# Layer 1's first gate-up part placed behind the second tile's transposes, the third tile's transposes inside it

## Chip, cores and metric

One of the cores of a Trainium2 chip runs the whole program. The metric is the device time of one execution in microseconds (us). A core has five engines with their own instruction streams: PE (matmuls and transposes), DVE and ACT (element by element), POOL (here: splitting the weights), and SP (here: starting transfers). They meet only through semaphores.

## What is computed

Two layers over 512 latent tokens and 256 context tokens of 1024 channels. What the change touches is the start of the feed-forward half of a layer:

```python
x = post_norm(x, g1 * y_l, ln1_w[layer], ln1_b[layer])
x = post_norm(x, g2 * swiglu(modulate(x, sh2, sc2), w_gate_up[layer], w_down[layer]),
              ln2_w[layer], ln2_b[layer])

def modulate(x, shift, scale):
    return layer_norm(x) * (1.0 + scale) + shift
def swiglu(h, w_gu, w_dn):
    g, u = jnp.split(h @ w_gu, 2, axis=-1)
    return (jax.nn.silu(g) * u) @ w_dn
```

`w_gate_up` is 1024 x 5632. The second and last layer (layer 1) computes this for the latent tokens only.

## The kernel before

**Tiles.** Tokens go in tiles of 128. Layer 0 has six of them, layer 1 in its feed-forward half four (here called first to fourth, numbered 0 to 3 in the code). Each fp32 product is made of three matmuls (`product`, L658 to L660): high by high, low by high, high by low half of the operands. Weights arrive in `stage`, POOL splits them into the eight slots of `ring_hi` (L623) and `ring_lo` (L626), and the last product that reads a slot raises `ring_used`, which lets POOL fill it again.

**From the norm to the operand.** After the output projection each tile goes through a chain over three engines. DVE adds the residual and norms twice (L1739 to L1812). ACT writes the normed tile `xn` (L1305). PE transposes it in eight blocks of 128 x 128 into two banks (`transposes`, L755). ACT modulates it into `hbuf` (L1313); for the last two tiles DVE does half of this (L1773). ACT writes the high half `act_hi` (L1321) and DVE the low half `act_lo` (L1730), and DVE then raises `low_ready`. PE's `wait_low(pe, key, n)` waits for that of tile n. `xn`, the two banks and `hbuf` are shared by the tiles, so the transposes of tile n wait for `xn` of tile n and for the modulation of tile n - 1. On ACT the order is fixed: modulation of tile n, square root of tile n + 1, high half of tile n, `xn` of tile n + 1.

**The start of gate-up.** `gate_up(l, 0)` (L1098) works on the first two blocks f = 0, 1 of 128 hidden columns in parts of 256 tokens (two tiles), `part(f, r, last)` (L1130): 8 gate products and then 8 up products, 48 matmuls. In layer 1 there are two token ranges r = 0, 1 and so four parts, in the order (f, r) = (0,0), (1,0), (0,1), (1,1), called first to fourth part. Before the parts with f = 0 PE waits for the low half of the second tile of their range: the second tile for the first part, the fourth tile for the third part. Transposes of the first tile stand in the last pass of the output projection (`last_pass`, L1076). Behind the parts come the blocks f = 2, 3, ... for all 512 tokens (`chunk`, L1104). Only parts with r = 1 raise `ring_used`. PE's order is the order in which this code is written; nothing passes a waiting instruction.

**ACT behind the norm.** After the fourth tile's high half, ACT issues two DMAs for the next norm's weights (L1558, L1559) and two for modulation weights (L1594), loads the table for silu and waits for the third part.

Of the kernel before, what the change touches and what calls it, by code (L numbers as in the profile page):

```python
# [136 lines left out]
def build(nc, x, c, ctx_in, c_ctx, w_mod, b_mod, w_in, a_q_norm, a_k_norm, b_sink, f_mix, r_decay,  # L137
# [3 lines left out]
    with stack:  # L141
# [111 lines left out]
        def sem(*name):  # L253
            key = "_".join(str(n) for n in name)
            if key not in sems:
                sems[key] = stack.enter_context(nc.semaphore(key))
            return sems[key]
# [16 lines left out]
        def tiles_of(l):  # L274
            return ALL if l < DEPTH - 1 else LAT
# [55 lines left out]
        def gates_done(l, seg):  # L331

            return GATE_OUT[(l, seg, 1)] + streams_of((l, seg, 1))
# [14 lines left out]
        def gate_banks(l, fh, f):  # L348

            parts = len(token_parts(l))  # L350
            if f % 2:
                return slice(2, 2 + parts), slice(4, 4 + parts)
            return slice(6, 6 + parts), slice(0, parts)
# [8 lines left out]
        def sum_bank(l, fh, f):  # L362

            return gate_banks(l, fh, f)[1].stop - 1

        def part_place(l, f, gu, r):

            c0 = r * 256 + (0 if l < DEPTH - 1 else CTX)
            return ps[:, r + f * len(tiles_of(l)) // 2, gu * 256:gu * 256 + 256], slice(c0, c0 + 256)
# [69 lines left out]
        def ffn_acc(half, n):  # L439

            items = FFN_MODS[half]
            return n % 3 if half == (0, 1) else 0 if items[n][1] != "modC" else 1 + items[n][2]

        def ffn_sum_chunk(half, n):

            last = max(f for f in range(HALF) for _, m, _, part in FFN_WHEN[half][f] if m == n and part == 3)
            return last + 2
# [5 lines left out]
        def ffn_units_to(half, n):  # L453

            return max(u for f in range(HALF) for u, m, _, _ in FFN_WHEN[half][f] if m == n) + 1
# [8 lines left out]
        def wait_low(e, key, n):  # L464

            need(e, "low_ready", key, n + 1)

        def shared_modulation(key, n):

            return n >= len(tiles_of(key[0])) - 2  # L470
# [29 lines left out]
        def need(e, name, l, n):  # L500

            before = NORMS[:NORMS.index(l)] if isinstance(l, tuple) else range(l)
            e.wait_ge(sem(name), n + sum(signals(name, k) for k in before))
# [151 lines left out]
        def _(pe):  # L655
            def product(o, a_hi, a_lo, b_hi, b_lo, first, last):

                nc.tensor.matmul(o, a_hi, b_hi, start=first, stop=False)  # L658
                nc.tensor.matmul(o, a_hi, b_lo, start=False, stop=False)  # L659
                return nc.tensor.matmul(o, a_lo, b_hi, start=False, stop=last)  # L660
# [32 lines left out]
            def column_sums(item, acc, bank, col):  # L693

                n = streams_of(item)
                for q in range(4):
                    for o in range(n):
                        mm = nc.tensor.matmul(ps[:, bank, col + n * q + o:col + n * q + o + 1], acc[:, o, q * P:(q + 1) * P],
                                              ones[:, :], start=(q + o == 0), stop=True, skip_group_check=True)
                mm.then_inc(col_out, 1)  # L700
# [45 lines left out]
            def transposes(key, n):  # L746

                need(pe, "xn_ready", key, n + 1)
                if n > 0:
                    need(pe, "h_ready", key, n)  # L750
                    if shared_modulation(key, n - 1):
                        nt = len(tiles_of(key[0]))
                        need(pe, "h_half", key, signals("h_half", key) - (nt - n))
                for k in range(KC):
                    mm = nc.tensor.transpose(ps[:, 6 + k // 4, (k % 4) * P:(k % 4 + 1) * P], xn[:, n % 2, k * P:(k + 1) * P],  # L755
                                             ident[:, :])
                mm.then_inc(sem("xn_T"), 1)
# [340 lines left out]
            def gate_up(l, fh):  # L1098
                lo_col, width, parts = (0, 384, 2) if l < DEPTH - 1 else (CTX, 512, 1)
                seg = f"gu{fh}"  # L1100
                g0 = SLOT0[(l, seg)]
                f0 = fh * HALF

                def chunk(g, f):  # L1104

                    if f >= 2:
                        need(pe, "hid_ready", l, f0 + f - 1)
                    elif f == 1:
                        need(pe, "dn_read", l, 2 * len(tiles_of(l)))
                    for n, item in enumerate(FFN_MODS[(l, fh)]):  # L1110
                        if item in COL_NO and ffn_sum_chunk((l, fh), n) == f:
                            pe.wait_ge(ffn_mod_used, ffn_units_to((l, fh), n))
                            column_sums(item, mod_acc_ffn[:, ffn_acc((l, fh), n), :, :], sum_bank(l, fh, f), 384 + 16 * (COL_NO[item] % 2))
                    for j in range(4):
                        pe.wait_ge(w_ready, g + j + 1)
                        for q in range(2):
                            k = 2 * j + q
                            for gu in range(2):
                                w = slice(q * 256 + gu * P, q * 256 + (gu + 1) * P)
                                wh, wl = ring_hi[:, (g + j) % RING, w], ring_lo[:, (g + j) % RING, w]  # L1120
                                for r in range(parts):
                                    bank = gate_banks(l, fh, f)[gu].start + r
                                    if f == 0 and k == 0 and gu and l < DEPTH - 1:
                                        need(pe, "dn_read", l, len(tiles_of(l)) + bank + 1)
                                    o = ps[:, bank, 0:width]
                                    s = slice(lo_col + r * width, lo_col + (r + 1) * width)
                                    mm = product(o, wh, wl, act_hi[:, k, s], act_lo[:, k, s], k == 0, k == 7)
                        mm.then_inc(ring_used, 1)

                def part(f, r, last):  # L1130

                    for gu in range(2):
                        o, s = part_place(l, f, gu, r)
                        for j in range(4):
                            g = g0 + 4 * f + j
                            pe.wait_ge(w_ready, g + 1)
                            for k in (2 * j, 2 * j + 1):
                                w = slice(k % 2 * 256 + gu * P, k % 2 * 256 + (gu + 1) * P)
                                mm = product(o, ring_hi[:, g % RING, w], ring_lo[:, g % RING, w], act_hi[:, k, s], act_lo[:, k, s],
                                             k == 0, k == 7)  # L1140
                            if last and gu:
                                mm.then_inc(ring_used, 1)

                if fh == 0:
                    key, nt = (l, 1), len(tiles_of(l))
                    n_parts = nt // 2
                    for n in ([1, 2] if n_parts == 2 else []):
                        transposes(key, n)
                    rest = list(range(3, nt))
                    steps = [(f, r) for r in range(n_parts) for f in range(2)]  # L1150
                    for f, r in steps:
                        if f == 0:
                            wait_low(pe, key, 2 * r + 1)
                            need(pe, "wout_read", l, nt + min(nt, r + n_parts + 1))
                        part(f, r, r == n_parts - 1)
                        if rest:
                            transposes(key, rest.pop(0))
                else:
                    pe.wait_ge(gate_read, gates_done(l, "modC"))
                for f in range(0 if fh else 2, HALF):  # L1160
                    chunk(g0 + 4 * f, f)
# [1074 lines left out]
```

## Time and profile before

| | us |
|---|---|
| median of three runs | 1818.13 (1816.22 to 1820.87) |
| the profiled execution | 1817.81 |
| its span | 1816.0 |
| PE busy | 1695.2 |
| DVE busy | 874.5 |
| POOL busy | 792.0 |
| ACT busy | 459.4 |

Times in the rows below count from the start of the span. A timeline row has start and duration in us, engine, line, operation, result <- operands, their shapes, and how many instructions are merged; in square brackets the idle time of the engine before it and the instruction that ended it. A wait row has who waited for whom, total us, number of waits, the longest. In rows by stretch "PEclk" is the granted clock of PE, 1.00 being the full one (2.4 GHz) and 0.50 the lower one (1.2 GHz). The time from the start of one matmul to the start of the next is what it costs in a dense stream; its duration in the row is longer, since matmuls overlap.

### The profile page before, as it was taken

The page shows a single profiled execution, that of the slowest core. Times are in us where ns is not written, and L with a number is a line of the kernel's source. Part 1 is how long each engine was busy: PE and PEld are TensorE (multiplying, and loading weights), DVE is VectorE, ACT ScalarE, POOL GpSimd, SP SyncE. Part 2 cuts the span into 40 slices and gives each one's busy share as a digit, 9 for nine tenths or more (in the row PEclk, how much of TensorE's full clock was granted, in tenths as well). Part 3 has the DMA queues.
Part 4 walks back from the last instruction along what each step waited for, and adds up shares of the span by engine and source line. Part 5 has one row for each costly group of instructions (what it writes and reads, how often), then busy time and mean ns, then how long its engine had stood idle before and what let it go on. Part 6 is the DMA issues. An engine that isn't in the chain of part 4 may idle for free. (4 is left out here: it accounts for less than half of the span.)

```text
span 1816.0 us, 23167 instructions
## 1 busy us (share of the span) xinstructions
PE 1695.2 (93%) x9198; PEld 1381.8 (76%) x9198; DVE 874.5 (48%) x1264; ACT 459.4 (25%) x956; POOL 792.0 (44%) x780
## 2 busy tenths in 40 slices
PE   5999899999899999999999969898999699999997
PEld 3887666557799997799998758685727688778885
DVE  4353244656862513554454684734476621340048
ACT  5411465521600002100002153126531400210021
POOL 3443001511464543544444444520143497677772
PEclk8999899999989999999999989999999899999999
DMA  9111034302162411244642211210112363233321
GB/s 358 55 57 60 20 127 152 96 1 70 48 185 82 128 60 46 70 123 133 192 156 72 64 46 42 75 47 17 49 50 70 93 174 104 82 93 93 100 98 47
DMA packets 157297, 164.96 MB, mean 91 GB/s; under 512 B 6414, under 2 KB 111742, under 8 KB 156934
## 3 DMA queue, kind: packets, MB, share of 16 engines
q1 hardware_dynamic: 136566, 121.40, 21.6%
q10 hardware_dynamic: 20624, 42.09, 7.0%
q8 instruction: 73, 1.20, 0.3%
q14 instruction: 34, 0.28, 0.1%
HBM read 161.37 MB, written 2.10 MB: 90 GB/s over the span
## 5 line engine op out<-in xcount | busy, mean ns | idle before, releaser
L623 POOL TENSOR_SCALAR ring_hi<-stage 128x512 fp32r<-128x512 f32 x368 | 266.6, 725 | 708.6 <-PE ps L660 680.9
L626 POOL TENSOR_TENSOR ring_lo<-stage,ring_hi 128x512 fp32r<-128x512 f32 x368 | 510.1, 1386 | 30.7
L658 PE MATMUL ps<-act_hi,ring_hi 128*128 128x384 f32 (+2 forms) x1168 | 405.4, 347 | 0.6 <-POOL ring_lo L626 0.6
L659 PE MATMUL ps<-act_lo,ring_hi 128*128 128x384 f32 (+2 forms) x1168 | 403.1, 345 | 0.0
L660 PE MATMUL ps<-act_hi,ring_lo 128*128 128x384 f32 (+2 forms) x1168 | 402.9, 345 | 0.0
L658 PE MATMUL ps<-ring_hi,act_hi 128*128 128x512 f32 (+1 forms) x748 | 298.8, 400 | 17.7 <-DVE act_lo L1730 9.1
L660 PE MATMUL ps<-ring_hi,act_lo 128*128 128x512 f32 (+1 forms) x748 | 291.4, 390 | 0.0
L659 PE MATMUL ps<-ring_lo,act_hi 128*128 128x512 f32 (+1 forms) x748 | 291.2, 389 | 0.0
L658 PEld LDWEIGHTS ps<-act_hi,ring_hi 128*128 128x128 f32 x1168 | 222.5, 190 | 13.9 <-POOL ring_lo L626 0.8
L659 PEld LDWEIGHTS ps<-act_lo,ring_hi 128*128 128x128 f32 x1168 | 222.4, 190 | 12.9
L660 PEld LDWEIGHTS ps<-act_hi,ring_lo 128*128 128x128 f32 x1168 | 222.2, 190 | 13.1
L658 PEld LDWEIGHTS ps<-ring_hi,act_hi 128*128 128x128 f32 x748 | 143.1, 191 | 56.7 <-issue 16.8
L2094 DVE TENSOR_TENSOR hid<-silu_g,ps 128x768 f32<-128x768 f32 (+1 forms) x44 | 36.1, 821 | 308.6 <-ACT silu_g L1580 308.4
L1580 ACT ACTIVATE silu_g<-ps 128x768 f32<-128x768 f32 (+1 forms) x44 | 31.0, 706 | 566.9 <-PE ps L660 525.1
L660 PEld LDWEIGHTS ps<-ring_hi,act_lo 128*128 128x128 f32 x748 | 142.8, 191 | 29.1
L659 PEld LDWEIGHTS ps<-ring_lo,act_hi 128*128 128x128 f32 x748 | 143.2, 191 | 26.9 <-issue 0.5
L1929 DVE SCALAR_TENSOR_TENSOR mod_acc_ffn<-mod_stage,c_silu,mod_acc_ffn 128x512 f32<-128x512 f32 x140 | 131.0, 960 | 26.8 <-DMA mod_stage<-in_w_mod_dram 23.7
L635 POOL TENSOR_TENSOR act_lo<-o_nrm,act_hi 128x128 fp32r<-128x128 f32 x40 | 18.1, 454 | 256.4 <-ACT act_hi L1434 256.4
L1958 DVE TENSOR_REDUCE negmax<-ps 128x1 f32<-128x768 f32 (+4 forms) x80 | 58.0, 766 | 94.3 <-PE ps L874 57.8
L1730 DVE TENSOR_TENSOR hs_lo<-hid,hs_hi 128x768 fp32r<-128x768 f32 (+1 forms) x44 | 59.0, 1341 | 80.1 <-ACT hs_hi L1567 72.1
L658 PE MATMUL ps<-ring_hi,hs_hi 128*128 128x512 f32 x220 | 88.0, 400 | 4.1 <-DVE resid L1741 3.1
L659 PE MATMUL ps<-ring_lo,hs_hi 128*128 128x512 f32 x220 | 86.7, 394 | 0.0
(216 smaller groups left out, 1957.9 us busy)
## 6 DMA issues: line engine op xcount, KB each, us to landing
stage<-in_w_gate_up_dram SPq DMA_DIRECT2D x88, 512.0 KB, 5.0
mod_stage<-in_w_mod_dram ACTq DMA_DIRECT2D x56, 512.0 KB, 4.2
stage<-in_w_in_dram SPq DMA_DIRECT2D x18, 1024.0 KB, 5.1
stage<-in_w_down_dram SPq DMA_DIRECT2D x16, 1024.0 KB, 4.9
stage<-in_w_mod_dram SPq DMA_DIRECT2D x12, 1024.0 KB, 5.3
start_mod<-in_w_mod_dram SPq DMA_DIRECT2D x8, 1024.0 KB, 12.2
stage<-in_w_down_dram SPq DMA_DIRECT2D x8, 768.0 KB, 4.3
stage<-in_w_out_dram SPq DMA_DIRECT2D x16, 256.0 KB, 4.6
```

The lines of the kernel that those rows point to most:

```text
L623: nc.gpsimd.tensor_scalar(ring_hi[:, g % RING, :], stage[:, par, j * 512:(j + 1) * 512], 1.0, 0.0, ALU.mult, ALU.add).then_inc(w_hi, 1)
L626: nc.gpsimd.tensor_tensor(ring_lo[:, g % RING, :], stage[:, par, j * 512:(j + 1) * 512], ring_hi[:, g % RING, :].bitcast(F32), ALU.subtrac ...
L635: nc.gpsimd.tensor_tensor(act_lo[:, ch, c], o_nrm[:, i % 2, :], act_hi[:, ch, c].bitcast(F32), ALU.subtract).then_inc(sem("o_lo"), 1)
L658: nc.tensor.matmul(o, a_hi, b_hi, start=first, stop=False)
L659: nc.tensor.matmul(o, a_hi, b_lo, start=False, stop=False)
L660: return nc.tensor.matmul(o, a_lo, b_hi, start=False, stop=last)
L1580: ins = a.activation(silu_g[:, e, lo_col:TOK].rearrange("p (r n) -> p r n", r=parts if fh or f > 1 else len(tiles_of(l)) // 2), gate_acc(l ...
L1730: return v.tensor_tensor(dst, src, high.bitcast(F32), ALU.subtract)
L1929: return v.scalar_tensor_tensor(acc, w, c_k, acc, ALU.mult, ALU.add)
L1958: v.tensor_reduce(negmax[:, m:m + 1], flat[:, 0:n], AX, ALU.max, negate=True).then_inc(sem("neg_ready"), 1)
L2094: done(v.tensor_tensor(hid[:, j, lo_col:TOK].rearrange("p (r n) -> p r n", **pat), silu_g[:, e, lo_col:TOK].rearrange("p (r n) -> p r n", ...
```

## The change

In layer 1 PE no longer does the third tile's transposes before the first part, but between its gate and its up products. The fourth tile's transposes, which stood behind the first part, now stand behind the second part, right ahead of the wait of the third part. `n_parts` is 2 in layer 1 and 3 in layer 0, where the order stays.

```diff
-                def part(f, r, last):
+                def part(f, r, last, split_at=None):
 
                     for gu in range(2):
+                        if gu and split_at is not None:
+                            transposes((l, 1), split_at)
                         o, s = part_place(l, f, gu, r)
...
                     n_parts = nt // 2
-                    for n in ([1, 2] if n_parts == 2 else []):
-                        transposes(key, n)
+                    if n_parts == 2:
+                        transposes(key, 1)
                     rest = list(range(3, nt))
                     steps = [(f, r) for r in range(n_parts) for f in range(2)]
                     for f, r in steps:
                         if f == 0:
                             wait_low(pe, key, 2 * r + 1)
                             need(pe, "wout_read", l, nt + min(nt, r + n_parts + 1))
-                        part(f, r, r == n_parts - 1)
-                        if rest:
+                        part(f, r, r == n_parts - 1, 2 if n_parts == 2 and f + r == 0 else None)
+                        if rest and (n_parts == 3 or f):
                             transposes(key, rest.pop(0))
```

## Rows read from the trace of the kernel before

**Rows 1.** The page, busy time of each engine, share, instructions.

```profile
PE 1695.2 (93%) x9198; PEld 1381.8 (76%) x9198; DVE 874.5 (48%) x1264; ACT 459.4 (25%) x956; POOL 792.0 (44%) x780
```

**Rows 2.** Waits of PE, 1400 to 1460.

```profile
PE ps L755 <- ACT xn L1305: 15.9, 2, 8.3
```

**Rows 3.** Timeline of PE, 1415 to 1457.

```profile
1420.39 1.97 PE L755 MATMUL ps<-ident_r,xn 128*128 128x128 f32 x8 [8.28 <-ACT xn L1305]
1429.95 1.97 PE L755 MATMUL ps<-ident_r,xn 128*128 128x128 f32 x8 [7.59 <-ACT xn L1305]
1431.57 0.56 PE L658 MATMUL ps<-act_hi,ring_hi 128*128 128x256 f32 x1
1431.93 0.42 PE L659 MATMUL ps<-act_lo,ring_hi 128*128 128x256 f32 x1
...
1434.07 0.31 PE L660 MATMUL ps<-act_hi,ring_lo 128*128 128x256 f32 x1
1434.22 0.28 PE L658 MATMUL ps<-act_hi,ring_hi 128*128 128x256 f32 x1
...
1438.53 1.03 PE L755 MATMUL ps<-ident_r,xn 128*128 128x128 f32 x8
1439.32 0.36 PE L658 MATMUL ps<-act_hi,ring_hi 128*128 128x256 f32 x1
...
1456.66 0.40 PE L658 MATMUL ps<-act_hi,ring_hi 128*128 128x512 f32 x1
```

**Rows 4.** The chain of waits in order of time (start, us, what), 1427 to 1431.

```profile
1427.01 1.24 DVE act_lo L1730
...
1428.66 1.25 ACT xn L1305
```

**Rows 5.** By stretch: length, busy time of the engines, PEclk, DMA share, GB/s.

```profile
1456.60:1750.00 293.40, 290.43 (x1269) 236.83 (x1269) 75.33 (x83) 33.92 (x57) 217.23 (x217) 1.00 0.36 108
```

**Rows 6.** Waits of PE from 1456.6 to the end, the largest.

```profile
PE ps L658 <- DVE resid L1741: 2.0, 2, 1.4
```

**Rows 7.** Timeline of POOL, its first split after the pause.

```profile
1449.07 0.62 POOL L623 TENSOR_SCALAR ring_hi<-stage 128x512 fp32r<-128x512 f32 x1 [22.39 <-PE ps L660]
```

**Rows 8.** By stretch, behind the restart at 1429.95.

```profile
1429.95:1434.15 4.20, 4.20 (x20) 4.20 (x21) 4.06 (x9) 1.68 (x5) 0.00 (x0) 0.50 0.45 119
1434.15:1438.50 4.35, 4.35 (x38) 4.35 (x38) 1.91 (x5) 2.19 (x2) 0.00 (x0) 1.00 0.00 0
```

**Rows 9.** By stretch, behind other restarts of PE.

```profile
38.00:41.60 3.60, 3.59 (x9) 2.86 (x10) 2.03 (x2) 3.57 (x6) 3.52 (x3) 0.52 1.06 381
479.20:485.30 6.10, 6.09 (x29) 6.09 (x30) 5.82 (x8) 4.03 (x10) 3.71 (x3) 0.51 0.16 49
1145.60:1149.00 3.40, 3.40 (x20) 3.00 (x21) 3.19 (x10) 0.49 (x1) 0.00 (x0) 1.00 0.00 0
1236.70:1239.60 2.90, 2.90 (x9) 1.23 (x10) 0.00 (x0) 0.00 (x0) 0.00 (x0) 0.51 0.00 0
```

**Rows 10.** Timeline of PE, those restarts with the idle time before them.

```profile
38.01 0.77 PE L658 MATMUL ps<-ring_hi,act_hi 128*128 128x512 f32 x1 [4.10 <-DVE act_lo L1730]
479.21 1.97 PE L755 MATMUL ps<-ident_r,xn 128*128 128x128 f32 x8 [2.91 <-ACT xn L1305]
1145.57 0.55 PE L772 MATMUL ps<-ident_r,post 128*128 128x128 f32 x3 [2.83 <-DVE post L1855]
1236.67 2.93 PE L874 MATMUL ps<-qk_A 64*128 64x512 f32 x8 [4.35 <-ACT probs L1409]
```

**Rows 11.** Timeline of ACT, 1434 to 1452.

```profile
1435.57 1.23 ACT L1305 ACTIVATE xn<-resid,st 128x1024 f32<-128x1024 f32 x1
...
1443.00 1.28 ACT L1580 ACT_TABLE_LOAD   x1 [0.80 <-issue]
1451.10 0.60 ACT L1580 ACTIVATE silu_g<-ps 128x512 f32<-128x512 f32 x1 [6.83 <-PE ps L660]
```

**Rows 12.** Timeline of DVE, the fourth tile's low half.

```profile
1442.30 1.23 DVE L1730 TENSOR_TENSOR act_lo<-hbuf,act_hi 128x1024 fp32r<-128x1024 f32 x1 [1.27 <-ACT act_hi L1321]
```

## Prediction

> **What bounds the kernel now.** I read the page's busy times first. The reader is to see there one engine near its limit: PE is busy for 93% of the span, DVE, ACT and POOL for at most half [rows 1]. So what counts is where PE stands still or runs at its lower clock, and whether the change alters either. Second, the waits of PE round the start of layer 1's gate-up: two waits for ACT's xn, 15.9 us together [rows 2]. Third, PE's own timeline. The second tile's transposes start at 1420.39 after 8.28 us of idling, the third's at 1429.95 after 7.59 us more; then 192 matmuls of 256 columns (four parts of 48) run without a break, the fourth tile's transposes among them, to 1456.66 [rows 3]. Fourth, the chain of waits: the third tile's transposes hang on xn, which ACT writes from 1428.66 to 1429.91, and that hangs on DVE, which worked on the second tile's low half until 1428.25 [rows 4]. That low half is what the first part needs, and nothing of part one needs the third tile. So PE holds back a part that could start at 1428.3 in order to do transposes that are ready at 1429.95. Behind 1456.66 PE is busy for 290.43 of 293.40 us at full clock [rows 5].
>
> **The change part by part.** Layer 0 has three parts a block and gets neither the split nor another place for its transposes, so its instruction stream stays. In layer 1 nothing is added or removed: the same 192 matmuls and 32 transposes, no DMA, no new tile. Two groups of eight transposes change places, and with them the waits that they carry. Call the tiles first to fourth.
>
> *The first part moves ahead of the third tile's transposes.* It waits for the second tile's low half, which ends at 1428.25 [rows 4]; PE starts within 0.05 us of a release here (xn ends 1429.91, transposes start 1429.95). So it starts at about 1428.3, not at 1429.95 as PE's work does now: 1.65 us gained. Its weights are long there, since POOL sits idle for 22.39 us before 1449.07, with all eight ring slots filled [rows 7]. Bounds: nothing in the rows before this point is touched, so I keep 1.5 to 1.7.
>
> *The clock at that start.* The granted clock is 0.50, the lower of the two levels, from PE's restart at 1429.95 to about 1434.2, and 1.00 behind [rows 8]. Lower-level cost from rows 3: eight transposes take 1.62 (1429.95 to 1431.57) against 0.79 (1438.53 to 1439.32) later; the first 12 matmuls take 2.65 (1431.57 to 1434.22) against 12 x 0.120 = 1.44. Loss now: 0.83 + 1.21 = 2.0. (0.120 is (1456.66 - 1439.32)/144; at the lower level one takes 0.214, (1434.07 - 1431.93)/10.) A stretch at the lower level thus loses 1 - 0.120/0.214 = 0.44 of its length. After other idle stretches the lower level lasted 2.9, 3.6 and 6.1 us from the restart, and 4.3 here [rows 8 to 10]. I take 3.6, from the restart that like the new one begins with full matmuls and not with transposes, for both restarts of the changed kernel: 1.6 lost each time. At the front that is 0.4 less than now. Bounds: 2.9 gives 1.3 (0.7 less than now), 6.1 gives 2.7 (0.7 more).
>
> *The third tile's transposes stand between gate and up products.* They start at 1428.3 + 24 x 0.120 + 1.6 = 1432.8, 2.8 later than now, when xn has been there since 1429.91. They cost their 0.79, counted already. Who waits for them: ACT's and DVE's modulation of the third tile, and queued behind ACT's, the fourth tile's square root and xn. All of it moves by about 2, so that xn of the fourth tile, now 1435.57 to 1436.80 [rows 11], would be there by 1439; it is wanted at 1442.2. Cost nothing, cover 3 us. If that cover were gone, the fourth tile's transposes would come later by what is missing, with PE idle for it.
>
> *The fourth tile's transposes lose their cover.* Now they stand between part one and part two. In the changed kernel they are issued behind part two, and the very next instruction is the third part, which waits for the fourth tile's low half. Now the transposes start at 1438.53 and the low half ends at 1442.30 + 1.23 = 1443.53 [rows 3, 12], so the chain of transposes, modulation on ACT and DVE, high half, low half is 5.00 long. Now part two (5.8) lies over it and part three starts with no wait. After the change the transposes start at 1428.3 + 96 x 0.120 + 0.79 + 1.6 = 1442.2, low is ready at 1447.2, PE is through with its eight at 1443.0: PE stands for 5.00 + 0.05 - 0.79 = 4.3. ACT and DVE have finished the third tile by then and have nothing else to do, so the chain is queued behind nothing and doesn't get shorter. Behind the waiting matmul stand, in PE's order, the whole of parts three and four and all later chunks; nothing can pass. POOL waits for part three's ring releases, and SP's weight loads for POOL; both shift along. On ACT's queue stand, behind the fourth tile's high half, four DMA issues and the table load for silu, now 1443.00 to 1444.28, with the first silu at 1451.10 [rows 11]: they move by 3.7, and so does that silu, so their 6.8 us of cover stay. Bounds: 3.9 to 4.7, an allowance of 0.4 either way on a chain of four steps that has been read once.
>
> *The clock after that stall.* Idle stretches of PE and what followed [rows 9, 10]: 2.83 idle, then 1.00; 2.91 idle, then 0.51; 4.10 idle, then 0.52; 4.35 idle, then 0.51. The new stall of 4.3 is nearest to the last two, so I take a fall, with 3.6 at the lower level: +1.6. Bounds 0 (no fall) to 2.7.
>
> The Trainium skill bears on this term, against the change: its page "TensorE: Matmul & The Clock Gate", section "Why this matters for your kernels", asks for no gaps of idle time between bursts of matmuls, since the gap takes the clock back to half. By that rule the term stands; without it the sum would be 2.2. The trace agrees in three of four gaps.
>
> Sum: -1.65 (earlier start) - 0.4 (front at lower clock) + 4.3 (stall) + 1.6 (clock behind it) = +3.85. As times: parts end at 1428.3 + 192 x 0.1204 + 2 x 0.79 + 1.6 + 4.3 + 1.6 = 1460.5 against 1456.66. What comes after is PE-bound [rows 5]; the longest group of PE's waits in it is 2.0, on residuals for which PE itself releases DVE [rows 6], so nearly all of the shift reaches the end.
>
> The profiled execution took 1817.81 (span 1816.0 and 1.8 round it), 0.3 under the median 1818.13. So 1821.6 in its terms and 1821.9 as median.
>
> **Rivals.**
> *A: the clock stays up over the stall.* For: 2.83 idle left it at 1.00 [rows 9, 10]. Against: the two gaps of 4.1 and 4.35. Gives +2.2, 1820.3.
> *B: both restarts are long ones (slower by over 0.3%).* One mechanism, the clock: at both restarts the lower level lasts 6.1, as after the restart at 479.21 [rows 9, 10], so that part one and the transposes in it run at the lower level altogether, and most of part three too. 3.85 + 1.1 + 1.1 = +6.0, 1824.1. It decides from about 5 us of lower level at both. For: seen once. Against: that restart began with transposes, and 2.9, 3.6 and 4.3 are more frequent.
> *C: the stall does not come up (not slower).* The third part finds the fourth tile's low half ready, or its wait bears on less than I read. Then -1.65 - 0.4 = -2.05, 1816.1. It decides where the chain is below 0.8 instead of 5.0. For: the front's gain is real. Against: each link of the chain has its row, and the wait stands in the code for the third part.
> *D: transposes inside the part run at the lower level.* The eight between gate and up product would take 1.62, not 0.79: 3.85 + 0.83 = +4.7, 1822.8. (The fourth tile's would lengthen chain and stall by what PE works more, so they add their 0.83 at most once more, 1823.6.) Against: the eight at 1438.53, in the middle of dense matmuls, took 0.79 [rows 3].
> The Trainium skill, same page, section "Part 4: PE-mode transpose", says that the full clock is not engaged by transposes. By that rule D would hold; the rows at 1429.95 (1.97 for eight, granted 0.50) and 1438.53 (1.03, granted 1.00) [rows 3, 8] show that transposes do run faster at the granted 1.00, so D stays small.
>
> **How the numbers follow.** Forecast 0.63, A 0.17, B 0.11, C 0.04, D 0.05. The median is from runs that spread from 1816.22 to 1820.87, so some 1.5 either way lies on each. A measurement of this kernel tells a change from about 0.3%, 5.45 us. Slower by more: most of B (0.08), and of the forecast and D the part that lies 1.6 above its value (0.09): 0.17. Faster by more needs -5.45, which no case reaches: 0.02. Within: 0.81. The range goes from A less a spread of the median (1818.7) to B plus a little (1825).
>
> **What would show it.** In the changed trace: first-part matmuls from about 1428.3; no wait of PE for xn of the third tile; transposes of the fourth tile right behind the second part; then a wait of PE for DVE's act_lo of about 4.3 us, a new row; granted clock 0.50 for some 3 to 4 us behind it; matmuls of 512 columns from 1460.5. The prediction is wrong in its mechanism if no such wait appears, and in a size if the chain from the transposes to the low half is not 5.0 or the lower level lasts otherwise.

## Result and profile after

The changed kernel takes 1822.16 us in the median of 18 runs (1819.31 to 1828.35), the kernel before 1818.08 in 18 runs of the same occasions (1815.16 to 1824.99). The ratio is 1.0021, 95% interval 1.0011 to 1.0031: slower by 4.1 us. The interval lies above 1, so the kernel is slower; the size is below the 0.3% from which the prediction counted a change, though the top of the interval lies just over it. Forecast were 1821.9 and +3.85. The profiled execution of the changed kernel has a span of 1819.1.

Spans of single executions scatter by more than the effect: the first tile's transposes, ahead of everything that was changed, start anywhere from 1408.21 to 1416.37 in the twelve profiles of this document. So I compare stretches inside the executions. First the waits of PE in the changed kernel round the start of gate-up, 1400 to 1470 (who waited for whom, total us, times, longest), to be read against [rows 2]. The kernel's line numbers are two higher than before from the new lines on: L1307 is xn, L1732 act_lo.

```profile
PE ps L658 <- DVE act_lo L1732: 10.0, 2, 5.9
PE ps L755 <- ACT xn L1307: 8.3, 1, 8.3
```

Before there were two waits for xn and none for act_lo. One of the two went (7.59), and two waits for low halves came, 5.94 and 4.01. The timeline of PE shows where, against [rows 3]:

```profile
1417.53 1.97 PE L755 MATMUL ps<-ident_r,xn 128*128 128x128 f32 x8 [8.28 <-ACT xn L1307]
1425.43 0.58 PE L658 MATMUL ps<-act_hi,ring_hi 128*128 128x256 f32 x1 [5.94 <-DVE act_lo L1732]
...
1430.72 1.24 PE L755 MATMUL ps<-ident_r,xn 128*128 128x128 f32 x8
1431.71 0.36 PE L658 MATMUL ps<-act_hi,ring_hi 128*128 128x256 f32 x1
...
1440.42 1.03 PE L755 MATMUL ps<-ident_r,xn 128*128 128x128 f32 x8
1445.47 0.58 PE L658 MATMUL ps<-act_hi,ring_hi 128*128 128x256 f32 x1 [4.01 <-DVE act_lo L1732]
...
1459.76 0.40 PE L658 MATMUL ps<-act_hi,ring_hi 128*128 128x512 f32 x1
```

From the second tile's transposes PE works again after 7.90 us (1425.43 - 1417.53); before it was 9.56 (1429.95 - 1420.39). That is the earlier start, 1.66. The fourth tile's transposes start at 1440.42 and the third part at 1445.47, 5.05 later. From the second tile's transposes to the first matmul of 512 columns it takes 42.23 us against 36.27 before, so this one execution lost 5.96 here. Behind it nothing has changed: 1819.1 - 1459.76 = 359.3, before 1816.0 - 1456.66 = 359.3. That the whole span grew by 3.1 only is because this execution reached the place 2.86 earlier. The stretches with their granted clock (third number from the end), against [rows 5, 8]:

```profile
1425.40:1430.70 5.30, 5.27 (x24) 5.27 (x25) 4.55 (x8) 1.24 (x1) 0.00 (x0) 0.50 0.70 193
1430.80:1440.40 9.60, 9.60 (x81) 9.60 (x80) 2.91 (x7) 3.77 (x7) 0.00 (x0) 0.98 0.00 0
...
1445.50:1451.20 5.70, 5.70 (x27) 5.70 (x28) 0.00 (x0) 0.68 (x1) 0.00 (x0) 0.50 0.95 284
1451.30:1459.70 8.40, 8.40 (x71) 8.40 (x71) 2.46 (x3) 0.60 (x1) 7.19 (x8) 0.98 0.12 34
1459.70:1753.10 293.40, 290.43 (x1269) 236.82 (x1269) 75.37 (x83) 33.93 (x57) 217.48 (x217) 1.00 0.37 108
```

The clock is at 0.50 over the whole gate product of the first part and rises only at 1431.1, inside the third tile's transposes, 5.7 us after the first restart; after the second it rises at 1451.6, 6.1 us later. Behind the parts PE's busy time is the same to a hundredth (290.43). DVE, ACT and POOL, against [rows 12, 11, 7], in three views:

```profile
1434.73 1.23 DVE L1732 TENSOR_TENSOR act_lo<-hbuf,act_hi 128x1024 fp32r<-128x1024 f32 x1 [0.59 <-ACT act_hi L1323]
...
1444.19 1.23 DVE L1732 TENSOR_TENSOR act_lo<-hbuf,act_hi 128x1024 fp32r<-128x1024 f32 x1 [1.27 <-ACT act_hi L1323]
```

```profile
1434.52 1.24 ACT L1307 ACTIVATE xn<-resid,st 128x1024 f32<-128x1024 f32 x1
...
1444.89 1.28 ACT L1582 ACT_TABLE_LOAD   x1 [0.81 <-issue]
1454.20 0.60 ACT L1582 ACTIVATE silu_g<-ps 128x512 f32<-128x512 f32 x1 [8.02 <-PE ps L660]
```

```profile
1452.17 0.62 POOL L623 TENSOR_SCALAR ring_hi<-stage 128x512 fp32r<-128x512 f32 x1 [28.35 <-PE ps L660]
```

The fourth tile's xn is there at 1435.76, 4.7 us before its transposes, so the move of the third tile's transposes held nothing up. Its low half ends at 1445.42, and PE starts 0.05 later. POOL is idle six us longer: it waits for PE. The first silu comes later too, after 8.02 us of waiting for PE instead of 6.83, so the cover of what stands ahead of it on ACT has grown.

### The profile page after: what moved, and what is told of

The parts are those of the page before. It is cut to its first block and busy times, and to the rows that moved or that the text cites. A ratio compares the mean times of both kernels' runs of the same rounds, so it can differ in the third digit from the quotient of the medians.

```text
span 1819.1 us, 23167 instructions
## 1 busy us (share of the span) xinstructions
PE 1696.9 (93%) x9198; PEld 1383.9 (76%) x9198; DVE 873.8 (48%) x1264; ACT 459.6 (25%) x956; POOL 792.1 (44%) x780
## 5 line engine op out<-in xcount | busy, mean ns | idle before, releaser
L1732 DVE TENSOR_TENSOR hs_lo<-hid,hs_hi 128x768 fp32r<-128x768 f32 (+1 forms) x44 | 59.0, 1342 | 80.1 <-ACT hs_hi L1569 72.2
```

The costliest lines, as they stand in the source:

```text
L1732: return v.tensor_tensor(dst, src, high.bitcast(F32), ALU.subtract)
```

## Experiments

The theory: the fourth tile's chain (transposes, modulation, high half, low half) has lost its cover and stands on PE's path, and the idle time costs a second time through the clock. The rival: the third tile's transposes inside the first part do the harm. For each kernel the table has the time from the first tile's transposes to the first matmul of 512 columns in its one profile, and the ratio to the kernel before over all runs, the kernel before having been measured again beside each. A stretch is one execution: the two of the changed kernel differ by 1.4 us, so smaller differences between two rows count only where the timeline says what they are made of. The expectations count from the second tile's transposes; the difference to the table is 9.3 us, except in the kernels with extra matmuls at the front, of which more below.

| kernel | stretch, us | less before | ratio, 95% interval |
|---|---|---|---|
| before | 45.58 | | |
| the change | 51.55 | +5.97 | 1.0021, 1.0011 to 1.0031 |
| after_again | 50.11 | +4.53 | 1.0033, 1.0021 to 1.0044 |
| late_alone | 53.00 | +7.42 | 1.0041, 1.0027 to 1.0055 |
| t3_back | 44.88 | -0.70 | 1.0001, 0.9986 to 1.0016 |
| t3_mid | 46.01 | +0.43 | 1.0002, 0.9991 to 1.0013 |
| t3_inside | 43.67 | -1.91 | 0.9974, 0.9960 to 0.9987 |
| t3_inside2 | 43.67 | -1.91 | 0.9980, 0.9970 to 0.9990 |
| busy_stall | 47.97 | +2.39 | 1.0015, 1.0001 to 1.0028 |
| warm_before | 43.91 | -1.67 | 0.9996, 0.9979 to 1.0013 |
| warm_best | 43.53 | -2.05 | 0.9985, 0.9972 to 0.9998 |
| warm_fuller | 42.49 | -3.09 | 0.9977, 0.9963 to 0.9991 |

**late_alone: one half of the change.**

```diff
 # the kernel before
-                        if rest:
+                        if rest and (n_parts == 3 or f):
                             transposes(key, rest.pop(0))
```

> The kernel before with one edit: the fourth tile's transposes behind the second part; the third tile's stay ahead of the first part. Theory (exposed chain): PE stands for 4.3 us before the third part and restarts at the lower clock for 3 to 6 us, so +4.3 +1.3 to +2.7 = +5.6 to +7.0 against before, ratio 1.0031 to 1.0039, slower than the full change, which also has an earlier start. Rival (the split inside the first part is what costs): no wait of PE for act_lo here, ratio 1.000. From the second tile's transposes to the first 512-column matmul: 36.3 before, 42 to 43.3 by the theory.

The loss is there without the split: 1825.66 against 1818.31 for the kernel before. In the stretch it is +7.42, more than the change's +5.97 and +4.53. PE at the third part:

```profile
1446.99 1.03 PE L755 MATMUL ps<-ident_r,xn 128*128 128x128 f32 x8
1452.03 0.58 PE L658 MATMUL ps<-act_hi,ring_hi 128*128 128x256 f32 x1 [4.01 <-DVE act_lo L1730]
```

The same 5.04 from transposes to third part and 4.01 idle. The place of the fourth tile's transposes alone makes the kernel slower; the rival falls. The third and fourth parts took 14.21 us (1452.03 to 1466.24) where 96 matmuls at 0.120 are 11.56, so 2.65 went to the lower clock, as expected. Its 53.00 lies 0.4 over the expected top, and that comes from the front: the first and second parts took 13.25 (1433.74 to 1446.99) where they took 6.96 + 48 x 0.120 = 12.74 before, since the lower clock lasted 5.3 us from the third tile's transposes instead of 4.2. Together 4.25 + 2.65 + 0.5 = 7.4.

**t3_back: the other half.**

```diff
 # the changed kernel
-                        if rest and (n_parts == 3 or f):
+                        if rest:
                             transposes(key, rest.pop(0))
```

> The changed kernel with the fourth tile's transposes back behind the first part, so only the split and the earlier start are left. Theory: no wait of PE for act_lo before the third part. The transposes now wait for the fourth tile's xn, which came 5.04 us after the start of the third tile's transposes, while PE has 3.9 us of work there: a wait of 1.2 us. The first part starts 1.65 sooner. So -1.65 + 1.2, and -0.7 to +0.7 for the clock at the front: -1.2 to +0.3, ratio 0.9993 to 1.0002; the stretch 35.1 to 36.6 us. Rival (the split costs): +4 and the stretch about 40.

PE in the changed place:

```profile
1432.01 1.04 PE L755 MATMUL ps<-ident_r,xn 128*128 128x128 f32 x8
1432.80 0.36 PE L658 MATMUL ps<-act_hi,ring_hi 128*128 128x256 f32 x1
...
1436.90 1.09 PE L755 MATMUL ps<-ident_r,xn 128*128 128x128 f32 x8 [0.99 <-ACT xn L1307]
1437.74 0.36 PE L658 MATMUL ps<-act_hi,ring_hi 128*128 128x256 f32 x1
```

No cost of the split shows: 1819.01 against 1818.31, interval 0.9986 to 1.0016. Its earlier start is partly eaten by the wait for the fourth tile's xn, whose transposes start 1.2 us later than PE's work would have let them (1432.80 + 24 x 0.120 = 1435.69), as expected from the chain ahead. With it neither half of the rival's claim is left.

**t3_inside: cover on both sides.** The fourth tile's transposes after 12 of the second part's 24 gate matmuls.

```diff
 # the changed kernel, inside part, after the matmuls of j
+                            if inside is not None and gu == 0 and j == 1:
+                                transposes((l, 1), inside)
...
-                        part(f, r, r == n_parts - 1, 2 if n_parts == 2 and f + r == 0 else None)
-                        if rest and (n_parts == 3 or f):
+                        part(f, r, r == n_parts - 1, 2 if n_parts == 2 and f + r == 0 else None,
+                             3 if n_parts == 2 and (f, r) == (1, 0) else None)
+                        if rest and n_parts == 3:
```

Here j counts the four ring slots of a product, six matmuls each.

> The changed kernel with the fourth tile's transposes inside the second part, after 12 of its 24 gate matmuls. Theory: xn is there (5.04 after the third tile's transposes start; PE arrives after 5.3), and behind them PE has 36 matmuls = 4.3 us and its own 0.8, against a chain of 5.0: both waits gone. Only the earlier start is left: -1.65, and -0.7 to +0.7 for the clock: -2.4 to -0.9, ratio 0.9987 to 0.9995; the stretch 34 to 35.4 us. Rival (the split costs, or the fourth tile's place is of no matter): as the change, ratio 1.002.

> The same as t3_inside, again on this chip beside the others: stretch 34.4 us, ratio 0.996 to 0.999. The first time gave 0.9974, more than the 1.9 us that its profile shows in the changed stretch; if that is scatter of the runs, this one comes out near 0.999.

```profile
1431.89 1.03 PE L755 MATMUL ps<-ident_r,xn 128*128 128x128 f32 x8
...
1437.08 1.04 PE L755 MATMUL ps<-ident_r,xn 128*128 128x128 f32 x8
1437.87 0.36 PE L658 MATMUL ps<-act_hi,ring_hi 128*128 128x256 f32 x1
```

No wait is left behind the start of the first part, and the medians are 1814.76 and 1815.23 against 1818.31 and 1818.73, both intervals below 1: faster than before and than the change. The stretch gives -1.9 both times, inside the expected range; the medians give -3.5, of which the second interval (-1.8 to -5.5) just holds the 1.9 and the first does not: its ratio of 0.9974 missed the expected 0.9987 to 0.9995. In both profiles what lies behind the stretch takes 359.4 as before, and ahead of it nothing was changed, so no place is left in which the edit could gain the rest. That the rest is scatter is likely and not shown.

**t3_mid: half the cover.** The fourth tile's transposes between gate and up products of the second part.

```diff
 # the changed kernel, inside part, ahead of part_place; the call as in t3_inside
+                        if gu and inside is not None:
+                            transposes((l, 1), inside)
```

> The changed kernel with the fourth tile's transposes between gate and up products of the second part. Theory (the stall is the chain less the work behind the transposes): the chain of 5.05 has 0.79 + 24 x 0.120 = 3.7 of PE's work over it, so the third part waits 1.4 us instead of 4.3, and so short a gap leaves the granted clock at 1.00. Stretch from the second tile's transposes to the first 512-column matmul: 34.4 (with the transposes inside the gate products) + 1.4 = 35.8 us; against before -0.5, ratio 0.999 to 1.0005. Rival (any place behind the second part's start costs the same): 42 us.

```profile
1439.68 1.04 PE L755 MATMUL ps<-ident_r,xn 128*128 128x128 f32 x8
1440.47 0.36 PE L658 MATMUL ps<-act_hi,ring_hi 128*128 128x256 f32 x1
...
1444.73 0.39 PE L658 MATMUL ps<-act_hi,ring_hi 128*128 128x256 f32 x1 [1.15 <-DVE act_lo L1735]
```

Again 5.05 from transposes to third part, whatever stands between; 1.15 of it idle. Behind this short gap the two parts took 11.62 us (1444.73 to 1456.35), full clock. The stretch is 0.9 longer than expected, from the front: there the whole gate product ran at the lower clock (1427.56 to 1432.85, 5.29) where t3_inside took 4.56, and the transposes behind it took 0.99 instead of 0.79.

**busy_stall: the clock's share of the stall.** The changed kernel with 30 matmuls in the stall, whose result is not used.

```diff
 # the changed kernel
+                def keep_busy(n):
+
+                    for _ in range(n):
+                        nc.tensor.matmul(ps[:, 1, 0:256], ring_hi[:, g0 % RING, 0:P], act_hi[:, 0, 0:256], start=True, stop=True)
...
                             transposes(key, rest.pop(0))
+                            if n_parts == 2:
+                                keep_busy(30)
```

> The changed kernel with 30 matmuls of 256 columns more, whose result in bank 1 is not used, between the fourth tile's transposes and the wait of the third part (3.6 us, inside the stall). Theory on the clock: PE doesn't idle, so the granted clock stays at 1.00 and the third part runs at 0.120 us a matmul; the stall itself remains. Gain over the change 1.3 to 2.7: against before +1.3 to +2.8, ratio 1.0007 to 1.0015. Rival A of the prediction (the clock doesn't fall anyway, or its fall costs nothing): as the change, ratio 1.0021. If the 30 outlast the stall: more than 4.3 us between the transposes and the third part.

```profile
1447.67 1.03 PE L755 MATMUL ps<-ident_r,xn 128*128 128x128 f32 x8
1448.46 3.84 PE L1149 MATMUL ps<-act_hi,ring_hi 128*128 128x256 f32 x30
1452.72 0.38 PE L658 MATMUL ps<-act_hi,ring_hi 128*128 128x256 f32 x1 [0.43 <-DVE act_lo L1739]
...
1464.34 0.40 PE L658 MATMUL ps<-act_hi,ring_hi 128*128 128x512 f32 x1
```

The stall is the same 5.05 long, and behind it the parts take 11.62 us where the changed kernel takes 14.29 (1445.47 to 1459.76). So the clock's share is 2.67 in this pair of profiles, and 2.2 against the second profile of the change (below). The medians, 1820.26 against 1822.16 measured at another time, agree in direction and can't size it: the two intervals overlap. Rival A of the prediction falls.

In this profile and that of t3_back the part behind the stretch took 361.1 and 360.9 us; in the other ten it took 359.3 to 359.4. The timelines show where: 100 us further on the clock fell to 0.50 once more, for some 3.4 us (from 1573.7 and 1564.2), with PE busy for over 5 us since its last wait of 1.01. The other profiles have the same wait and keep the full clock. It lies outside the stretches, and adds 1.6 to those two spans.

**after_again: the changed kernel a second time.**

> The changed kernel once more, for a second profile. Theory: the wait of the third part for the fourth tile's low half is again 4.0 us, since it follows from the chain; the lower clock behind it again comes but may be shorter than the 5.9 us of the first profile (3 to 6); ratio 1.001 to 1.003. Rival (the 5.9 us are the rule): 5.9 again.

```profile
1430.20:1433.80 3.60, 3.60 (x17) 3.60 (x18) 3.34 (x6) 1.24 (x1) 0.00 (x0) 0.50 0.99 275
1434.00:1444.00 10.00, 10.00 (x86) 10.00 (x85) 3.91 (x10) 3.77 (x7) 0.00 (x0) 1.00 0.00 0
1449.40:1454.30 4.90, 4.90 (x23) 4.90 (x24) 0.00 (x0) 0.62 (x1) 0.00 (x0) 0.50 1.01 296
1454.60:1463.00 8.40, 8.40 (x73) 8.40 (x72) 2.46 (x3) 0.60 (x1) 7.15 (x8) 1.00 0.17 42
```

The idle time is 4.01 again. The lower clock lasted 3.6 at the front instead of 5.7, and 5.0 behind the stall instead of 6.1; at 0.44 lost of each us that is 1.4, the difference of the two stretches. The ratio of 1.0033 lies just over the expected 1.003, with an interval of 1.0021 to 1.0044. So the waits are fixed, and the clock's part varies from one execution to the next.

**warm_before, warm_best, warm_fuller: keep PE busy at the front.** Extra matmuls (keep_busy, behind a wait for ring slot g0) ahead of and behind the second tile's transposes; warm_fuller has 62 for the second number. warm_before is the kernel before with 60 and 56 of them.

```diff
 # t3_inside
+                        keep_busy(60)
                         transposes(key, 1)
+                        keep_busy(50)
```

> The kernel before with 60 and 56 matmuls of 256 columns more, result unused, in the idle stretches ahead of the second and of the third tile's transposes. Theory: the order stays, the third tile's transposes start when xn comes, the clock is at 1.00: stretch 36.3 - 2.0 = 34.3 us, ratio 0.9985 to 0.9995. Rival (the loss at the front is small or given back): 36.3 us, 1.000.

> The kernel with the fourth tile's transposes after 12 gate matmuls of the second part, and 60 and 50 matmuls of 256 columns more, whose result in bank 1 is not used, in the two idle stretches before and behind the second tile's transposes. Theory: the idle stretches keep their length from PE's view (the norm's chain sets them), the granted clock stays at 1.00 through them, the first part runs at 0.120 us a matmul from its start, and the stretch falls from 34.4 to about 32.6; ratio against before 0.9975 to 0.9985, 1.5 to 2.7 us below the same kernel without the extra matmuls. Rival (the lower clock at the front is free, because the tile chain covers it): equal to that kernel.

> As warm_best, but 62 instead of 50 extra matmuls between the second tile's transposes and the first part, so that PE's gap there shrinks from 1.8 to about 0.4 us. Theory: the granted clock fell to 0.50 for 3.4 us at the start of the first part because of that gap; without it the clock stays at 1.00 and 1.5 us go: from the first tile's transposes to the first 512-column matmul 42.0 to 42.3 us instead of 43.5. Rival (the fall has nothing to do with the gap): again 3.4 us at 0.50 in or near the first part, 43.5.

In all three the second tile's transposes come 8.3 us after the first's and not 9.3, but the low half after them comes no earlier: 17.16 from the first tile's transposes to the first part in warm_best and warm_fuller, 17.21 in t3_inside. Therefore the table counts from the first tile. warm_before shows no lower clock there and takes 1.6 less from the third tile's transposes on (25.11 against 26.71), of the 2.0 expected: the front's loss is real in the stretch, though not resolved in its median. It kept the full clock over 2.75 us of idle time:

```profile
1429.64 1.09 PE L755 MATMUL ps<-ident_r,xn 128*128 128x128 f32 x8 [2.75 <-ACT xn L1312]
1429.70:1436.50 6.80, 6.78 (x56) 6.58 (x56) 5.72 (x12) 4.00 (x7) 0.00 (x0) 1.00 0.35 93
```

warm_best missed, with 0.14 less than t3_inside where 1.8 was expected: the clock was at full level up to 1428.0 and fell there, with 1.83 idle before it.

```profile
1419.10:1428.00 8.90, 7.08 (x58) 6.87 (x58) 8.54 (x10) 4.46 (x11) 7.55 (x7) 1.00 0.26 70
1428.03:1431.50 3.47, 3.47 (x17) 3.47 (x18) 3.21 (x6) 1.24 (x1) 0.00 (x0) 0.53 1.04 285
```

warm_fuller, with 0.39 of idle time, stayed at 1.00:

```profile
1408.00:1427.00 19.00, 18.58 (x151) 17.96 (x150) 16.35 (x26) 10.57 (x24) 16.26 (x14) 1.00 0.25 68
1427.10:1431.00 3.90, 3.90 (x35) 3.90 (x35) 3.76 (x6) 1.46 (x4) 0.00 (x0) 1.00 0.74 203
```

It has the shortest stretch, 42.49, with 0.23 of it a new wait for the fourth tile's xn. Its median, 1814.39 against 1818.22, is not told apart from t3_inside's. That the gap of 1.83 brought the fall in warm_best rests on one pair of profiles, and the longer gap in warm_before brought none, so it is not shown.

## Why the prediction was right, and where a term was off

**Earlier start, 1.65.** Measured 1.66. PE followed the low half within 0.05, as taken.

**The third tile's transposes at no cost.** Right: t3_back and both t3_inside have the split and are not measurably slower. The fourth tile's xn came 4.7 us before it was wanted; the cover was put at 3.

**The stall, 4.3.** Measured 5.05 - 0.79 = 4.26 in both profiles of the change and 4.25 in late_alone. t3_mid and t3_inside show that it is the chain less what PE has to do behind the transposes: 1.4 left with 24 matmuls over it, none with 36.

**Clock behind the stall, 1.6.** It fell in three of three profiles with 4.0 idle (the change twice, late_alone) and not in t3_mid after 1.15. But it stayed down 5.0 to 6.1 us and not 3.6, and cost 2.7, 2.2 and 2.65 (14.29, 13.78 and 14.21 less 11.56). The term was 0.6 to 1.1 too small. The restart of 3.6 that I took as the nearest had been one of 512-column matmuls. The list of restarts that the term rests on was also not whole. The trace of the kernel before has one more, behind 3.06 us of idle time, where the lower clock lasted 9.5 us:

```profile
533.78 3.55 PE L698 MATMUL ps<-ones,mod_acc_ffn 128*128 128x1 f32 x16 [3.06 <-DVE mod_acc_ffn L1929]
533.80:543.30 9.50, 9.50 (x35) 9.50 (x36) 6.08 (x9) 0.81 (x1) 1.58 (x2) 0.50 0.81 235
```

With it the bound of 2.7 on this term was too low (by the prediction's own 0.44 lost of each us, 9.5 gives 4.2), long restarts had been seen twice and not once, and rival B deserved more than its 0.11. The Trainium skill ("TensorE: Matmul & The Clock Gate", "Why this matters for your kernels") warns of long idle gaps of PE between bursts of matmuls, since the clock goes back to half. The traces agree in these three; warm_best, where it was down after 1.83, does not fit a rule on long gaps.

**Clock at the front, -0.4.** Now +0.6 in the first profile: gate product 5.29 against 2.89 at full clock, and the transposes 0.99 against 0.79, so 2.6 lost where it had been 2.0. In after_again, at 4.56, it was 1.7, that is -0.3. The sign varies with the execution.

**Sum.** By the profile -1.66 + 0.6 + 4.26 + 2.7 = +5.9, which is the measured 5.96; that is rival B, the two long restarts, come true in one execution. after_again has +4.5, and the medians give +4.1 (interval 2.0 to 5.6) and, the second time, +5.8 (3.8 to 8.0). The forecast of 3.85 is at the low edge of the second interval and inside the first; a fair sum with the clock terms as measured is 4.5 to 6, close to the bound of 0.3%. So the stall and the earlier start were right in mechanism and size, the clock terms were too small by 0.7 to 2.1 together, and that the median came within 0.3 of the forecast is in part luck.

**Rivals.** A fell (granted 0.50 behind the stall in all three profiles that have one of 4.0 us idle, and busy_stall). C fell: the wait is there. D fell: eight transposes ahead of the up product took 0.79 (1432.01 to 1432.80) in t3_back once the clock was up. The Trainium skill, "TensorE: Matmul & The Clock Gate", section "Part 4: PE-mode transpose", says that the full clock doesn't engage for transposes; the rows differ, and the rows decide.

## What to carry to other kernels

An instruction that starts a chain over other engines should be placed by what waits at the chain's end: count the work of the issuing engine between the two, here 5.05 us of chain against 0.8, 3.7 and 5.1 of work, and put the start back by what is missing. When one such group is moved earlier or later, look for the next group that it pushes to the edge of its own cover; here the good half of the change (1.65) was lost to the other half, and 36 matmuls' difference in the place of eight transposes turned +4 into -3.5 in the medians and +4.5 to +6 into -1.9 in the stretch. Here the exposed wait counted one and a half times for PE: 4.26 of waiting cost 6.5 to 7 with the clock that it took along.

## What was not expected of the hardware

- The lower clock set in after as little as 1.83 us of idle time in warm_best and stayed for 3.5 us of dense matmuls, while 2.83 [rows 9, 10], 2.75 (warm_before) and 1.15 (t3_mid) left it up. In t3_back and busy_stall it came over 5 us after the last wait. Length of a gap alone doesn't tell.
- In the three kernels with extra matmuls at the front the 128x1 step of DVE that releases the second tile's xn took 0.25 us instead of 0.90, and xn came 1 us sooner. In either case the step ended with POOL's operation beside it: at 1418.10 in t3_inside (POOL's 1415.98 + 2.11 = 1418.09), at 1417.80 in warm_best (1416.10 + 1.69 = 1417.79). The rows fit a step of DVE that is held until POOL's operation ends. The time did not stay: that tile's low half took 2.08 instead of 1.23 in warm_best and came as late as without. Why the extra matmuls shift POOL against DVE is open.
